# Reordering VectorE and ScalarE work inside the delta-rule step of a two-layer decoder kernel

## The reference

```python
def delta_mixer(h, s0, conv_buf, w_in, conv_w, a_log, dt_bias, o_norm_w, w_out):
    proj = h @ w_in                                   # q, k, v, z, beta, a
    qkv, conv_new = causal_conv(qkv, conv_buf, conv_w)   # 4 taps, then SiLU
    ...
    lmat = jnp.einsum('nbhcd,nbhed->nbhce', kb, k) * decay_strict
    tmat = lax.linalg.triangular_solve(lmat + eye, jnp.broadcast_to(eye, lmat.shape),
                                       left_side=True, lower=True, unit_diagonal=True)
    u_base = jnp.einsum('nbhce,nbhef->nbhcf', tmat, v * beta[..., None])
    ...
    o = rmsnorm(o, o_norm_w) * jax.nn.silu(z)
    return o @ w_out
```

## Time and profile before

| | before |
|---|---|
| time, median of 3 runs | 2230.56 us (2230.39 to 2232.59) |
| time of the profiled execution | 2230.45 us |
| its span, first to last instruction | 2228.7 us |
| TensorE busy | 2146.4 us, 96% |
| VectorE busy | 1311.4 us, 59% |
| ScalarE busy | 840.1 us, 38% |
| GpSimd busy | 220.4 us, 10% |
| mean granted TensorE clock, share of full | 0.992 |
| length of one loop step (windows of 69.45 us repeat) | 69.45 us |

### The profile page before, as it was taken

One profiled execution on the slowest core, in us unless ns is written; L12 is line 12 of the kernel. 1 busy time (PEld: TensorE's weight loads), 2 busy tenths in 40 slices (PEclk: granted clock), 3 DMA queues, 4 the chain that ended last, 5 costly groups with the idle time before them and its releaser, 6 DMA issues.

```text
span 2228.7 us, 49903 instructions
## 1 busy us (share of the span) xinstructions
PE 2146.4 (96%) x18829; PEld 2060.9 (92%) x18829; DVE 1311.4 (59%) x2171; ACT 840.1 (38%) x1658; POOL 220.4 (10%) x313
## 2 busy tenths in 40 slices
PE   6999999999999999999999999999999999999998
PEld 4989889898898988899889999999999999999997
DVE  5566676666766667666675444554555656654443
ACT  4334433344333443333443333433333333343333
POOL 3012121121111211111111001000000000000010
PEclk9999999999999999999999999999999999999999
DMA  5534443544435444254434644444444444454442
GB/s 155 161 94 132 141 136 93 146 129 142 139 88 149 130 142 138 88 145 132 141 108 142 191 144 147 161 151 157 151 155 149 151 163 138 155 172 149 139 146 95
DMA packets 379977, 311.10 MB, mean 140 GB/s; under 512 B 19609, under 2 KB 375866, under 8 KB 379322
## 3 DMA queue, kind: packets, MB, share of 16 engines
q1 hardware_dynamic: 378042, 306.30, 45.0%
q10 hardware_dynamic: 1872, 3.96, 0.5%
HBM read 283.85 MB, written 27.25 MB: 140 GB/s over the span
## 4 chain that ended last, share of the span: by engine, by line
PE 86%; DVE 8%; issue 3%; ACT 1%; DMA 0%; DVEq 0%; ACTq 0%; SPq 0%; POOL 0%; POOLq 0%
PE ps L291 24%; PE ps L292 23%; PE ps L293 23%; PE ps L1121 12%; DVE s_s L1056 1%; PE ps L1288 1%; DVE dec L924 1%; DVE convout L915 1%; DVE silu L936 1%; DVE silu L938 1%; DVE amat L1066 0%; DVE wlo L282 0%; PE ps L1142 0%; DMA xtok<-in_x_sample_dram 0%; DVE ym L1011 0%
## 5 line engine op out<-in xcount | busy, mean ns | idle before, releaser
L291 PE MATMUL ps<-xhi,whi 128*128 128x320 f32 x3072 | 985.4, 321 | 23.6 <-ACT zraw L621 19.6
L293 PE MATMUL ps<-xhi,wlo 128*128 128x320 f32 x3072 | 951.4, 310 | 0.0
L292 PE MATMUL ps<-xlo,whi 128*128 128x320 f32 x3072 | 951.2, 310 | 0.0
L282 DVE TENSOR_TENSOR wlo<-wraw,whi 128x1024 fp32r<-128x1024 f32 (+1 forms) x484 | 584.7, 1230 | 218.7 <-ACT whi L277 216.2
L291 PEld LDWEIGHTS ps<-xhi,whi 128*128 128x128 f32 x3072 | 579.2, 189 | 47.0 <-DVE wlo L282 22.1
L277 ACT ACTIVATE whi<-wraw 128x1024 fp32r<-128x1024 f32 (+1 forms) x484 | 497.1, 1048 | 263.6 <-PE ps L293 237.7
L292 PEld LDWEIGHTS ps<-xlo,whi 128*128 128x128 f32 x3072 | 579.6, 189 | 0.9
L293 PEld LDWEIGHTS ps<-xhi,wlo 128*128 128x128 f32 x3072 | 578.8, 188 | 0.0
L293 PE MATMUL ps<-bhi,wlo 128*128 128x320 f32 x512 | 158.0, 309 | 0.0
L291 PE MATMUL ps<-bhi,whi 128*128 128x320 f32 x512 | 158.0, 309 | 0.0
L292 PE MATMUL ps<-blo,whi 128*128 128x320 f32 x512 | 158.0, 309 | 0.0
(11 more groups left out here) (332 smaller groups left out, 2379.1 us busy)
## 6 DMA issues: line engine op xcount, KB each, us to landing
wraw<-in_delta_w_in_dram SPq DMA_DIRECT2D x384, 256.0 KB, 3.2
wraw<-in_pool_w_in_dram SPq DMA_DIRECT2D x256, 256.0 KB, 3.0
wraw<-in_delta_w_out_dram SPq DMA_DIRECT2D x128, 256.0 KB, 3.3
wraw<-in_pool_w_out_dram SPq DMA_DIRECT2D x128, 256.0 KB, 3.2
s_s<-in_state_delta_dram SPq DMA_DIRECT2D x32, 512.0 KB, 6.4
out_dram<-s_s SPq DMA_DIRECT2D x32, 512.0 KB, 4.2
wraw<-in_pool_w_group_dram SPq DMA_DIRECT2D x64, 256.0 KB, 3.0
dec<-gc_rows SPq DMA_DIRECT2D x16, 320.0 KB, 4.2
```

Source lines behind the costliest of these rows:

```text
L282: nc.vector.tensor_tensor(wlo[:, slot, 0:width], wraw[:, slot, 0:width], whi[:, slot, 0:width].bitcast(F32), ALU.subtract).then_inc(E("w_l ...
L291: mm(o, whi[:, slot, w], hi[:, k_x, :], start=first, stop=False)
L292: mm(o, whi[:, slot, w], lo[:, k_x, :], start=False, stop=False)
L293: done = mm(o, wlo[:, slot, w], hi[:, k_x, :], start=False, stop=last)
```

## The change

Five edits, all of order or of engine; no arithmetic is added or removed.

1. VectorE, levels 1 to 5: the convolution tap (levels 1 to 4), `r4` and `o4` (level 3) and the decays (level 4) now stand between P's split and the X copy, not behind the X copy. The tap `conv_next(1, 0)` moves from level 5 to behind the two copies into `ym`.
2. The copy of `lp6` into `p6` moves from VectorE to ScalarE, ahead of ScalarE's `split(9)`. Two new semaphores, `x5` and `y_kept`, replace what VectorE's order gave.
3. ScalarE, steps 1 to 15: `z_evac` of the next head stands between the two tanh and the sample copies, not at the very end.
4. ScalarE, prologue: `silus(0)` stands ahead of `z_evac(0)`.
5. VectorE, prologue: two splits, half the convolution, two splits, the other half, two splits; before: six splits, then the whole convolution.

```diff
@@ delta_act @@
             sc.activation(silu[:, 2:4, :], convout[:, 2:4, :], ACT.Tanh, scale=0.5).then_inc(E("tanh"), 1)
+            if loop_of(i):
+                z_evac(i, i * 12 + (HEADS + 12))
             act.wait_ge(E("silu"), i + 1)
...
-                split(4 + k)
+                if k < 5:
+                    split(4 + k)
+            act.wait_ge(E("lp6"), n)
+            sc.activation(p6[0:64, :, :], blocks(D0[0:64, 0:256], 4), ACT.Copy).then_inc(E("p6"), 1)
+            split(9)
             act.wait_ge(E("xt6"), n)
...
+        silus(0)
         z_evac(0, HEADS + 12)
-        silus(0)
...
             delta(i, split, lambda i=i: cc_evac(i), lambda i=i: cc_store(i), lambda i=i: silus(i), lambda: None)
-            z_evac(i, i * 12 + (HEADS + 12))
@@ delta_dve @@
                 split(3 + k)
-                dve.wait_ge(E("lx"), (n - 1) * 5 + k)
-                if k == 1:
-                    v.tensor_copy(xc[:], blocks(D2[:, 0:320], 5))
-                else:
-                    v.tensor_copy(half_blocks(xc[:, 0:units, :], k, 0), packed(D2, units, k))
-                conv_next((k - 1) // 4, (k - 1) % 4)
-                if k == 4:
-                    decays_next()
+                if k < 5:
+                    conv_next(0, k - 1)
                 if k == 3:
...
+                if k == 4:
+                    decays_next()
+                dve.wait_ge(E("lx"), (n - 1) * 5 + k)
+                if k == 1:
+                    v.tensor_copy(xc[:], blocks(D2[:, 0:320], 5))
+                elif k < 5:
+                    v.tensor_copy(half_blocks(xc[:, 0:units, :], k, 0), packed(D2, units, k))
+                else:
+                    v.tensor_copy(half_blocks(xc[:, 0:units, :], k, 0), packed(D2, units, k)).then_inc(E("x5"), 1)
             dve.wait_ge(E("y5"), n)
             for h in range(2):
                 r = slice(64 * h, 64 * h + 64)
-                v.tensor_copy(ym[r, :, 64 * h:64 * h + 64], yc[r, :, :])
-            dve.wait_ge(E("lp6"), n)
-            v.tensor_copy(p6[0:64, :, :], blocks(D0[0:64, 0:256], 4)).then_inc(E("p6"), 1)
+                last = v.tensor_copy(ym[r, :, 64 * h:64 * h + 64], yc[r, :, :])
+            last.then_inc(E("y_kept"), 1)
+            conv_next(1, 0)
             split(9)
...
-        for j in range(8, 12 + LEAD):
+        for j in range(8, 10):
             split_lo(dve, HEADS + j, j % 4)
...
             for j in range(TAPS):
                 conv(0, half, j)
+            for j in (10, 11) if half == 0 else range(12, 12 + LEAD):
+                split_lo(dve, HEADS + j, j % 4)
@@ delta_pe @@
             pe.wait_ge(E("p6"), n)
+            pe.wait_ge(E("x5"), n)
...
             pe.wait_ge(E("y6"), n)
+            pe.wait_ge(E("y_kept"), n)
```

## The result

The changed kernel takes 2192.01 us (median of 4 runs, 2189.06 to 2192.85) against 2230.64 us for the kernel before (4 runs, 2230.39 to 2232.59): 38.6 us less, a ratio of 0.9823 with the interval 0.9806 to 0.984. Forecast were 2191.7 us. The profiled execution took 2192.85 us, with a span of 2191.1 us; its mean granted clock is 0.993 of full.

A forecast was written before the change was run, and what follows sets the result against it. TensorE, busy 96% of the span, was taken to bound the kernel with its waits. Removed stops of 22.6 us (levels, `p6`), 14.6 (`z_evac`) and 1.5 (prologue) sum to 38.7: 2230.45 - 38.7 = 2191.7 us, range 2184 to 2204.

The forecast's parts named there:

- Levels: Loop levels 3 and 5: TensorE's stops of 0.32 and 0.43 us waiting for P go in steps 1 to 15.
- The walk along VectorE: VectorE's new order followed through levels 3 to 5: P of level 5 ready by 297.4, 1.5 us in hand.
- no slack on X: Level 4: moved VectorE work ends near 296.5, and the X copy cannot begin before `lx`, also near 296.5.
- rival A: Levels 3 and 5 keep their stops because moved VectorE instructions delay X: 11 us missing, 2203 us; chance 0.09.
- 0.1 us in hand: Level 6: VectorE's tap pair ends at 305.3 and `u_m` is there at 305.41, the narrowest place of the change.
- rival C: Slower through `lp6`, `p6`, ScalarE's split, VectorE's split, tap pair, `ud`; at 4 us late about 2246 us; chance 0.04.
- Prologue: VectorE's reordered splits and convolution let TensorE finish `fill(4)` at 114.0 where today it is at 115.51: 1.5 us gained.
- I take them as lost again: Prologue: the 3 us lost to about 6 us at half clock stay lost; a kept clock would gain 3 us more.
- Nothing gained: Loop's exit: TensorE waits for the branch's low parts, not for z, so moving `z_evac` ahead gains nothing there.

The follow-up runs named there:

- the two doses: The changed kernel with two or three more pairs of unused tap-like instructions on VectorE behind the decays of level 4: 2191.85 us with two, 2195.31 us with three.

## Why the prediction was right

**Levels.** In the step shown the three stops are gone to the last hundredth, no wait row of theirs is left for the whole span, and edit 1 alone gave 11.6 us where the stops of levels 3 and 5 add up to 11.3. The walk along VectorE holds: shifted to the clock of the step shown before (7.11 us at level 3, where TensorE asks at 282.79 for 289.90), P of level 3 is over at 287.55 for 287.5, and the split at 290.10 for 290.1. By the Trainium skill's rule ("SBUF — State Buffer", "Who interferes with whom") it would be at 290.25; GpSimd's instruction is over at 281.91 here:

```profile
278.29 3.62 POOL L539 TENSOR_TENSOR s_s<-s_s,cur 128x2048 f32<-128x2048 f32 x1 [4.44 <-PE ps L1298]
```

and a whole split of 1.23 behind it would end at 283.14, where the row has 282.99. The rule is right as to what is held: the split, with two SBUF inputs, is, while the predicated copy, whose data come from PSUM, takes its 0.30 us in the middle of GpSimd's instruction. How the split comes to end 0.15 us earlier no run here tells.

**Room at level 5.** Here a size was off: "no slack on X" at level 4. VectorE is ready 1.00 us before `lx`. About half of that is `r4` and `o4`, which take 0.6 us together (283.89 to 284.48, with no idle time), not the 1.06 allowed; the rest is that successive instructions overlap a little in the rows (`o4` starts at 284.15, `r4` ends at 284.23) where the walk laid them end to end. The room that counts is 2.9 us, found with the two doses, so rival A deserved less than its 0.09.

**`p6`.** The copy runs from 0.68 us after `lp6` starts and takes 0.38, as said (293.01 to 293.69 to 294.07), and `y6` is not late. `ud` waits 0.39 us for `u_m`, more than the "0.1 us in hand". Nothing in the runs speaks for rival C. What the text did not see is that the same gain, all but 0.12 us a step, was to be had with the copy on VectorE: in the whole change the tap's new place is enough for most of it.

**`z_evac`.** 1.02 us a step for 1.04; 14 times that is 14.3, alone it gave 14.7 us.

**Prologue.** 1.5 us were predicted and by the traces 3.0 came (2.5 between the medians for the two edits alone). The stop was near the 3.6 us forecast (3.45) and sits ahead of `fill(4)`. "I take them as lost again" was wrong: the clock did fall, but for 3.4 us, not 6.8, and not over the same work. At the transposes 0.2 us were won in place of 1.5, because `fill(4)` lost 1.5 us at half clock (5.16 for 3.63); 2.8 us came back in step 1. This term was off by a factor of two, and the sum hardly shows it because it is small.

**Loop's exit.** "Nothing gained" was nearly right: TensorE waits there 3.72 us for the branch's low parts, before 4.04, and the trace of edit 3 alone shows that these 0.3 us are its doing. In the changed kernel's trace the clock is low for longer there. Its windows (0.50 in all that are left out):

```profile
1118.00:1119.00 1.00, 0.00 (x0) 0.89 1.05 295
...
1125.00:1126.00 1.00, 1.00 (x7) 0.70 0.00 0
```

That is 6.8 us (0.22 + 6 + 0.6). In the kernel before, the same place has 3.4 us, from

```profile
1159.00:1160.00 1.00, 0.79 (x4) 0.71 0.95 318
...
1162.00:1163.00 1.00, 1.00 (x6) 0.59 0.00 0
```

From the `cur` copy that follows in the timelines of DVE (at 1165.46 us before, at 1126.70 after) to the end of the span it takes 2228.7 - 1165.46 = 1063.2 us before and 2191.1 - 1126.70 = 1064.4 us after, 1.2 us more. That belongs to the run and not to the change. The kernel before with edits 4 and 5 alone, whose loop and exit are those of before, shows a low stretch of 6.8 us at this place and 1065.7 us to the end; the changed kernel with `p6` back on VectorE shows 3.4 us and 1063.5 us.

**Account.** By the traces: 15 x 1.47 = 22.1 us for the levels and `p6` (22.6 in the sum), 14.3 for z (14.6), 3.0 for the prologue (1.5) and 0.3 at the exit (none), together 39.7. The profiled executions differ by 37.6 us: the changed kernel's is 1.2 us longer behind the exit and comes 0.9 us later to the last big matmul ahead of the prologue's stop (107.19 for 106.26; over the kept traces this ranges from 105.49 to 109.44). The medians differ by 38.6. So the forecast was right stop by stop in the loop and gave the prologue half of what it was worth. That the medians meet the sum of 38.7 to 0.1 us is luck: four runs of the changed kernel spread over 3.8 us.

## What to carry to other kernels

When the busiest engine waits again and again for a short copy, look at what stands directly ahead of that copy on its engine, and put there only what is ready no later: moving a tap pair of 0.7 us out of the way was worth nearly as much as giving the copy to another engine. Walk once along the engine that is loaded with the moved work, with durations from rows (those of a stretch with the same neighbour on GpSimd, if there is one), and find out how far the new order is from its next stop: here 2.9 us a step. A stop of TensorE of 3 to 4 us has a second price in the stretch behind it, where the granted clock is at half, and that stretch differed by a factor of two between traces. So an edit that removes such a stop altogether is worth more than one that moves it.

## What was not expected of the hardware

The stretch of lower clock after a stop of TensorE does not simply follow the length of the stop. In the prologue it is 3.4 us behind stops of 2.78 to 3.48 us and 6.8 us behind stops of 3.56 and 4.28 us, in five traces each. But at the loop's exit the same stop of 3.72 us has 6.8 us behind it in three traces (the changed kernel's among them) and 3.4 in three others, and the one of 4.04 us has 3.4 in four and 6.8 in one. Behind the stop of 0.76 us there was none. What decides between the two no run here shows.

A VectorE copy with PSUM data and an SBUF mask, 0.30 us, was not held by a GpSimd instruction of 3.62 us that held the next instruction, a split with two SBUF inputs (2.65 us for 1.23).
